# A two-layer encoder with a routed mixture of experts: two weight loads put into the buffers of w_o, and two groups of small TensorE products put elsewhere in the router stage

## The chip, the core and the metric

The kernel runs on one core of a Trainium2 chip. The metric is the device time of one execution in microseconds (us). TensorE (PE) does the matmuls and the transposes, VectorE (DVE) and ScalarE (ACT) the elementwise work, GpSimd (POOL) issues the gathers, the scatters and some stores, and SyncE (SP) issues the loads of all large weights.

## The reference

Two layers (DEPTH = 2) over 512 tokens of width 1024, float32. Each layer is an attention mixer followed by a mixture of experts; the part around the change is the passage from the one to the other:

```python
x = x + g1 * hybrid_mixer(h, ...)            # ends in: merged @ w_o
h = rms_norm(x, norm2[l]) * (1.0 + sc2) + sh2
x = x + g2 * grouped_moe(h.reshape(B * S, D), w_router, router_bias, w1[l], w3[l], w2[l])
```

`grouped_moe` scores 16 experts for each token, takes the best two inside the best group of four, and adds up `(silu(xb @ w1[e]) * (xb @ w3[e])) @ w2[e]` with the normed scores as weights. The six modulation vectors (sh1, sc1, g1, sh2, sc2, g2) of a layer are products of `silu(c)` with `w_ada[l]`.

## The kernel before, in words

**Stages of a layer.** Norm and transposes, input projection, two attentions, gates, the product with w_o (L2012, eight groups k = 0 to 7 of eight matmuls, two halves of the columns for each of four token tiles t), the router, and then the experts in 11 passes (PASSES) of 128 token rows. All is written out by hand, engine by engine; each engine runs its own list in order and waits on semaphores.

**Between w_o and the first pass.** DVE adds the mixer's output to x (L1405), PE transposes x and makes the router's logits, ACT writes the last tile of the scaled x (L1101) and POOL stores each tile of it to the DRAM tensor `xn_d` (L860), 512 KB each; the gathers read it. DVE turns the logits into one-hots (L1466), PE adds them up to ranks (L2048 to L2050, semaphore `ranks_ready`), DVE makes from the ranks the 128-wide indicator rows of the first pass (L1489, eight of them), PE multiplies them with token numbers (`slot_table(1, ...)`, L2059, 16 matmuls of 2 columns), and DVE writes the result as an index list (L1503, L1504, semaphore `ft_s`). With it POOL gathers the first pass's tokens from `xn_d` (L869). DVE then orders the experts by their counts (L1514, semaphore `ord_s`, which SP waits for before it loads any expert that depends on the order) and makes the indicator rows for all passes (L1541, semaphore `ds_s`); PE multiplies them (`slot_table(PASSES, ...)`, L2059, 16 matmuls of 22 columns) and DVE writes the full index table (L1545, L1548, semaphore `tb_s`), with which POOL gathers passes 1 and 2 and later ones. For a gathered pass PE transposes the tokens (`token_transposes`, L2073, two groups of four), ACT scales and shifts them into `xsT` (L1110), and the up products follow (L2107), then the down products (L2118).

**Modulation columns.** In layer 0 alone, PE also makes the next layer's first two modulation vectors by 16 one-column products (`next_mod`, L2037; each float32 product stands in the trace as two instructions). DVE reads them at L1572.

**POOL's list** at this place: wait for the four stores (`xn_st`), wait for `ft_s`, wait for x (`x1`), gather 0; wait for `tb_s`, gathers 1 and 2.

**Weight buffers.** The ring has six buffers of 2 MB (0 to 5); `hT` and `reg_a`, when they are free, serve as buffers 6 and 7. `MOE_LOADS` lists all 48 loads of a layer as (place, matrix, buffer), matrix 0, 1, 2 for w1, w3, w2. The places 0 and 1 are two fixed experts, whose loads wait for nothing but the buffer; the other places are filled in the order of the counts. The two halves of w_o lie in buffers 4 and 5: groups k = 0, 2, 4, 6 read buffer 4 and k = 1, 3, 5, 7 buffer 5. `hT` is read by the router's partial logits (L1991). `wo_r` counts the groups of w_o that are done, `lp4_r` the tiles with partial logits.

Of the kernel before, what the change touches and what calls it, by code (L numbers as in the profile page):

```python
# [16 lines left out]
NT = SEQ // P  # L17
NC = D // P
# [33 lines left out]
PASSES = 11  # L52
STATIC = (11, 12)
# [15 lines left out]
def rows_by_rank():  # L69

    first, rows = [None] * E, [0] * E
    for p, tiles in enumerate(TILES):
        for j, at, n in tiles:
# [4 lines left out]

MOE_LOADS = ((0, 2, 0), (1, 0, 1), (1, 2, 2), (0, 0, 3), (0, 1, 5), (1, 1, 6),
# [7 lines left out]
MOE_SLOT = {(j, m): s for j, m, s in MOE_LOADS}  # L89

TR_N1, TR_QK, TR_LAT, TR_KR, TR_N2, TR_X0 = 0, 8, 13, 18, 28, 36
# [21 lines left out]
def gathers(b):  # L113
    return (PASSES + 1 - b) // 2
# [65 lines left out]
def trunk(nc, x_in, c_in, w_ada, b_ada, norm1, w_in, q_norm_a, k_norm_a, q_a_norm, kv_norm, w_q_b,  # L180
# [27 lines left out]
    with ExitStack() as ctx:  # L208
# [253 lines left out]
        wo_r = sem("mixer_out_ready")  # L462
# [56 lines left out]
        def wait(eng, s, value):  # L519

            eng.wait_ge(s, value)
            eng.sem_inc(ticks, 1)
# [23 lines left out]
        def _(sp):  # L546
# [31 lines left out]
            for l in range(DEPTH):  # L578
# [58 lines left out]
                def load_w1(j, e):  # L637
                    s = MOE_SLOT[j, 0]
                    sp.dma_start(slot(s, NC, F), w1_v[l * E + e]).then_inc(w_rdy[s], 16)

                def load_w3(j, e):
                    s = MOE_SLOT[j, 1]
                    sp.dma_start(slot(s, NC, F), w3_v[l * E + e]).then_inc(w_rdy[s], 16)
# [8 lines left out]
                load_w2(1, STATIC[1])  # L652
                wait(sp, yb_r, l * 8 + 8)
                load_w1(0, STATIC[0])
                wait(sp, wo_r, l * 8 + 8)
                load_w3(0, STATIC[0])
                wait(sp, lp4_r, l * NT + NT)
                load_w3(1, STATIC[1])

                wait(sp, ord_s, l + 1)  # L660
# [7 lines left out]
                wait(sp, xn_st, l * 64 + 64)  # L668
                load_w1(2, rank[2])
                wait(sp, xg_s[0], l * (16 * gathers(0)) + 16)  # L670
                load_w3(2, rank[2])
                rank[3] = expert_at(3)
                wait(sp, h1_r, l * PASSES + 1)
# [1027 lines left out]
        def _(pe):  # L1701
# [46 lines left out]
            for l in range(DEPTH):  # L1748
# [280 lines left out]
                def next_mod(first, end):  # L2029

                    if l < DEPTH - 1:
                        if first == 0:
                            pe.wait_ge(nu_s, l * NX + NX)
                            pe.wait_ge(x1, l * 8 + 8)
                        for i in range(first, end):
                            m, c = i // NC, i % NC
                            ins = pe.matmul(bank[7][:, i:i + 1], nx_acc[:, m * D + c:(m + 1) * D:NC],  # L2037
                                            ones[:, 0:1], start=True, stop=True)
                        if end == 2 * NC:
                            ins.then_inc(nm_r, 1)  # L2040
# [7 lines left out]
                    pe.matmul(bank[3][:, (t + 1) * E:(NT + 1) * E], ones_b, before(t, NT - t), start=t == 0, stop=False)  # L2048
                pe.matmul(bank[3][:, E:NT * E], utri_b, ra_b[:, E:NT * E], start=False, stop=True)
                pe.matmul(bank[3][:, 0:E], utri_b, ra_b[:, 0:E], start=True, stop=True).then_inc(rk_r, 1)  # L2050
                next_mod(5, 2 * NC)

                def slot_table(n, slots, per_token, slots_done, done):

                    for q in range(2 * NT):
                        if slots_done is not None:
                            pe.wait_ge(slots_done, l * (2 * NT) + (q + 1))
                        for w in (0, 2):
                            ins = pe.matmul(bank[2][:, 0:2 * n], slots[:, q, :], per_token[:, q, w:w + 2, :].rearrange("p w n -> p (w n)"),  # L2059
                                            start=q == 0 and w == 0, stop=q == 2 * NT - 1 and w == 2)  # L2060
                    ins.then_inc(done, 1)
                slot_table(1, first_slot, places_b, fs_s, ft_r)
                slot_table(PASSES, slot_of, chosen, ds_s, tp_r)

                def token_transposes(g, p0, b, first=False):

                    xv = xg[:, b, :].rearrange("p (q c) -> p c q", c=NC)
                    for k in range(2):  # L2070
                        pe.wait_ge(tr_e, g + (k - 1))
                        for c in range(4):
                            ins = pe.transpose(bank[(p0 + k) % 2][:, c * P:(c + 1) * P], xv[:, 4 * k + c, :], ident)  # L2073
                        ins.then_inc(tr_r, 1)
# [46 lines left out]

                pe.wait_ge(xg_s[0], l * (16 * gathers(0)) + 16)
                token_transposes(l * TR + TR_X0, 0, 0)
                for p in range(PASSES):
                    g = l * TR + (TR_X0 + 2 + 3 * p)
                    if p == 4:
                        most = rows_beyond(pe, l)
                    pe.wait_ge(tr_e, g - 1)
                    for m, done in ((0, h1_r), (1, h3_r)):
                        if p == PASSES - 1 and m == 1:  # L2130
                            pe.wait_ge(tr_e, g)
                            pe.wait_ge(y_e, (l * PASSES + p - 1) * 2)
                            down_tiles(p - 1)
                        for j in places(p):
                            loaded(j, m)
                        for c in range(NC):
                            if p == 0 and c == 4:
                                pe.wait_ge(tr_e, g)
                            ins = up_tiles(p, m, 4 + m, c)
                        ins.then_inc(done, 1)  # L2140
                    if p + 1 < PASSES:
                        pe.wait_ge(xg_s[(p + 1) % 2], l * (16 * gathers((p + 1) % 2)) + 16 * ((p + 1) // 2 + 1))
                        token_transposes(g, p % 2, (p + 1) % 2)
                    if p == 1:
                        pe.wait_ge(wa_s, l + 1)
                        for t in range(NT):
                            ins = pe.transpose(bank[2][:, t * P:(t + 1) * P], last_a[:, t, :], ident)
                        ins.then_inc(wt_r, 1)
                    if 1 <= p < PASSES - 1:
                        pe.wait_ge(tr_e, g)  # L2150
                        if p >= 2:
                            pe.wait_ge(y_e, (l * PASSES + p - 1) * 2)
                        down_tiles(p - 1)
                    pe.wait_ge(u_s_s, l * PASSES + p + 1)
                    gu = g + 2 if p + 1 < PASSES else g
                    pe.wait_ge(tr_e, gu - 1)
                    hidden_transposes(p % 2).then_inc(tr_r, 1)
# [46 lines left out]
```

## Time and profile before

| what | value |
|---|---|
| median of 3 runs | 1566.89 us (1565.07 to 1570.05) |
| profiled execution | 1566.08 us |
| its span, first to last instruction | 1563.8 us |
| PE busy | 1476.5 us, 94% |
| DVE busy | 580.3 us, 37% |
| ACT busy | 428.0 us, 27% |
| moved by DMA | 346.80 MB, mean 222 GB/s |

A share of the span says which engine has most to do over all stages, and not what a stage waits for; that is read from the chain of work that ended last and from the engines' timelines. In a row of a timeline the first number is the start in us from the span's start, the second how long the row lasts; behind it the idle time of the engine before it and what ended it. Layer 0's router stage lies at about 507 to 532 us, layer 1's at about 1264 to 1288 us.

### The profile page before, as it was taken

The numbers are of one execution on the slowest core, as the hardware profiler recorded it, in microseconds if no ns is written. First come the engines' busy times: TensorE is split into PE (matmuls) and PEld (weight loads), VectorE is DVE, ScalarE is ACT, GpSimd is POOL, SyncE is SP. The second block draws the span as 40 slices with busy tenths as digits, with TensorE's granted clock in tenths as the row PEclk, the third lists the DMA queues.
The fourth block names the chain that finished last, engine by engine and source line by source line (L and its number), as shares of the span: only waits on it lengthen the run. The fifth ranks groups of instructions, "written<-read, shape, count | busy, mean of one in ns | idle before, by whom it ended". The sixth has DMA issues, their size and how long they took to land.

```text
span 1563.8 us, 20111 instructions
## 1 busy us (share of the span) xinstructions
PE 1476.5 (94%) x7800; PEld 800.5 (51%) x7801; DVE 580.3 (37%) x1379; ACT 428.0 (27%) x988; POOL 86.8 (6%) x96
## 2 busy tenths in 40 slices
PE   4998999999999799999899899999999959999997
PEld 1564565677754433343346555666776433334333
DVE  0056654575742511111154464463333251111115
ACT  1326564400011121211142565551000121121112
POOL 0000002000000001010000000020000010111000
PEclk8999999999999699999999999999999979999999
DMA  9625163225181889999972442601203458999994
GB/s 361 236 83 190 56 205 119 86 76 162 54 306 49 312 354 396 415 422 419 375 294 108 137 137 74 197 1 41 81 27 128 168 210 325 405 408 421 424 414 193
DMA packets 94874, 346.80 MB, mean 222 GB/s; under 512 B 13738, under 2 KB 37898, under 8 KB 80376
## 3 DMA queue, kind: packets, MB, share of 16 engines
q1 hardware_dynamic: 69152, 305.68, 50.5%
q0 software_dynamic: 8976, 31.40, 5.5%
q10 hardware_dynamic: 16648, 8.40, 1.9%
q8 instruction: 64, 1.05, 0.3%
q14 instruction: 34, 0.28, 0.0%
HBM read 331.55 MB, written 21.00 MB: 225 GB/s over the span
## 4 chain that ended last, share of the span: by engine, by line
PE 87%; DMA 6%; ACT 2%; DVE 2%; issue 1%; SPq 0%; DVEq 0%; POOLq 0%; ACTq 0%
PE bank L2107 18%; PE bank L1844 12%; PE bank L1794 10%; PE bank L2118 9%; PE bank L2012 7%; PE bank L1886 7%; PE bank L1901 5%; PE bank L1911 4%; PE bank L1921 4%; DMA hT<-in_w 3%; PE bank L1827 2%; PE bank L1723 2%; PE bank L1758 2%; DMA ring<-in_w_ada 1%; PE bank L2073 1%
## 5 line engine op out<-in xcount | busy, mean ns | idle before, releaser
L2107 PE MATMUL bank<-ring,reg_b 128*32 128x512 f32 (+2 forms) x1440 | 283.7, 606 | 2.9 <-ACT reg_b L1110 2.9
L2107 PEld LDWEIGHTS bank<-ring,reg_b 128*32 128x32 f32 (+2 forms) x1440 | 95.4, 127 | 158.3 <-issue 154.1
L1794 PE MATMUL bank<-ring,hT 128*128 128x512 f32 (+3 forms) x512 | 159.1, 472 | 2.4 <-ACT hT L943 2.4
L2118 PE MATMUL bank<-ring,reg_b 128*32 128x512 f32 (+2 forms) x640 | 141.3, 594 | 6.7 <-DMA hT<-in_w 3.7
L1794 PEld LDWEIGHTS bank<-ring,hT 128*128 128x128 f32 x512 | 97.8, 192 | 59.1 <-issue 32.2
L1886 PE MATMUL bank<-reg_a,ring 128*128 128x512 f32 x256 | 112.6, 593 | 0.9 <-issue 0.9
L2012 PE MATMUL bank<-ring,reg_b 128*128 128x512 f32 x256 | 113.0, 596 | 0.0
L1110 ACT ACTIVATE reg_b<-bank,cur 128x128 f32<-128x128 f32 x176 | 63.7, 467 | 170.5 <-PE bank L2073 170.5
L1022 ACT ACTIVATE reg_f<-bank,nmax 128x512 f32<-128x512 f32 x128 | 87.0, 684 | 61.5 <-DVE nmax L1320 60.5
L1320 DVE TENSOR_REDUCE nmax<-bank 128x1 f32<-128x512 f32 x128 | 83.8, 686 | 50.9 <-PE bank L1901 50.9
L1844 PE MATMUL bank<-hT,ring 128*128 128x256 f32 x384 | 88.1, 379 | 0.0
L2118 PEld LDWEIGHTS bank<-ring,reg_b 128*32 128x32 f32 (+2 forms) x640 | 48.3, 128 | 76.7 <-issue 72.9
L1620 DVE TENSOR_TENSOR reg_d<-bank,reg_c 128x512 f32<-128x512 f32 x44 | 30.4, 692 | 138.6 <-PE bank L2118 138.4
L1844 PEld LDWEIGHTS bank<-hT,ring 128*128 128x128 f32 x384 | 72.8, 190 | 15.8 <-issue 6.7
L1921 PE MATMUL bank<-cst,reg_f 128*128 128x128 f32 x512 | 71.2, 281 | 6.7 <-DVE reg_f L1314 4.1
L1886 PEld LDWEIGHTS bank<-reg_a,ring 128*128 128x128 f32 x256 | 48.5, 190 | 55.6 <-issue 54.9
L2012 PEld LDWEIGHTS bank<-ring,reg_b 128*128 128x128 f32 x256 | 47.7, 190 | 56.3 <-issue 56.3
L1608 DVE TENSOR_TENSOR reg_b<-bank,reg_b 128x512 f32<-128x512 f32 x22 | 15.2, 692 | 164.8 <-ACT reg_b L1117 164.8
L2107 PE MATMUL bank<-hT,reg_b 128*32 128x512 f32 (+1 forms) x160 | 70.5, 593 | 0.0
L1314 DVE TENSOR_SCALAR reg_f<-reg_f,linv 128x512 f32<-128x512 f32 x128 | 66.2, 517 | 10.3 <-issue 0.4
L1921 PEld LDWEIGHTS bank<-cst,reg_f 128*128 128x128 f32 x512 | 55.0, 141 | 25.9 <-DVE reg_f L1314 16.3
L1613 DVE TENSOR_TENSOR reg_b<-bank,reg_b 128x512 f32<-128x512 f32 x22 | 15.2, 692 | 123.6 <-PE bank L2107 123.6
(301 smaller groups left out, 1839.3 us busy)
## 6 DMA issues: line engine op xcount, KB each, us to landing
ring<-in_w SPq DMA_DIRECT2D x72, 2048.0 KB, 17.1
ring<-in_w_ada SPq DMA_DIRECT2D x19, 2048.0 KB, 7.8
hT<-in_w SPq DMA_DIRECT2D x12, 2048.0 KB, 14.5
reg_a<-in_w SPq DMA_DIRECT2D x12, 2048.0 KB, 13.5
ring<-in_w_in SPq DMA_DIRECT2D x10, 2048.0 KB, 15.7
vb<-in_w_ada ACTq DMA_DIRECT2D x16, 512.0 KB, 4.0
ring<-in_w_o SPq DMA_DIRECT2D x4, 2048.0 KB, 9.7
ring<-in_w_proj_a SPq DMA_DIRECT2D x8, 512.0 KB, 11.5
```

What stands on the lines that cost most here:

```text
L1022: A(prob[:, u % 2, h, :], bank[4 + at][:, :], ACT.Exp, bias=nmax[:, at:at + 1], accum_out=lsum[:, at:at + 1]).then_inc(ex_s, 1)
L1110: ins = A(xsT[:, b, cc, :], bank[(p0 + k) % 2][:, c * P:(c + 1) * P], ACT.Identity, scale=scale2(cc), bias=shift2(cc))
L1314: TS(prob[:, u % 2, h, :], prob[:, u % 2, h, :], linv[:, at:at + 1], None, ALU.mult).then_inc(pn_s, 1)
L1320: v.tensor_reduce(nmax[:, at:at + 1], bank[4 + at][:, :], X, ALU.max, negate=True).then_inc(mx_s, 1)
L1794: ins = pe.matmul(bank[z_bank(k)][:, 0:n], hT[:, c, t * P:(t + 1) * P], w[:, c, :], start=c == 0, stop=c == NC - 1)
L1844: ins = pe.matmul(bank[bk][:, half * 256:(half + 1) * 256], w[:, c, :], tokens[:, c, :], start=c == 0, stop=c == 3)
L1886: ins = pe.matmul(branch_bank(j, q)[:, :], w[:, c, (j % 4) * P:(j % 4 + 1) * P], oT[:, c + 4 * q, :], start=c == 0, stop=c == 3)
L1901: pe.matmul(bank[4 + 2 * (u % 2) + h][:, :], q_of(k, h), k_of(k, h), start=True, stop=True).then_inc(s_r, 1)
L1921: ins = pe.transpose(bank[2 + h][:, kc * P:(kc + 1) * P], prob[:, u % 2, h, kc * P:(kc + 1) * P], ident)
L2012: ins = pe.matmul(wo_bank(k)[:, :], mT[:, c, t * P:(t + 1) * P], w[:, c, :], start=c == 0, stop=c == NC - 1)
L2107: ins = pe.matmul(bank[bk][at:at + n, :], xsT[:, p % 2, c, at:at + n], slot(MOE_SLOT[j, m], NC, F)[:, c, :], start=c == 0, stop=c == NC - 1)
L2118: ins = pe.matmul(bank[6 + h][at:at + n, :], uT[:, c, at:at + n], slot(MOE_SLOT[j, 2], 4, D)[:, c, h * 512:(h + 1) * 512], start=c == 0, s ...
```

## The change

Three edits.

1. **Fixed matrices.** w3 of fixed place 0 goes to buffer 4 instead of 5, w3 of fixed place 1 to buffer 5 instead of 6 (`hT`), and w3 of place 2 to buffer 6 instead of 4. The other entries follow by the same exchange of names (5 becomes 4, 6 becomes 5, 4 becomes 6), so that each load still takes the place of the same matrix as before. SP's waits follow: w3 of place 0 waits for seven groups of w_o and not eight, w3 of place 1 for eight groups and not for the partial logits, and w3 of place 2 waits for the partial logits as well as for gather 0.
2. **Modulation columns.** `next_mod(5, 2 * NC)` stands behind the first pass's table and not ahead of it.
3. **Full table.** The products of the full table stand behind `token_transposes` of the first pass and not ahead of it.

```diff
-MOE_LOADS = ((0, 2, 0), (1, 0, 1), (1, 2, 2), (0, 0, 3), (0, 1, 5), (1, 1, 6),
-             (2, 0, 7), (2, 1, 4), (3, 0, 3), (3, 1, 5), (2, 2, 1), (4, 0, 7),
+MOE_LOADS = ((0, 2, 0), (1, 0, 1), (1, 2, 2), (0, 0, 3), (0, 1, 4), (1, 1, 5),
+             (2, 0, 7), (2, 1, 6), (3, 0, 3), (3, 1, 4), (2, 2, 1), (4, 0, 7),
...
                 load_w1(0, STATIC[0])
+                wait(sp, wo_r, l * 8 + 7)
+                load_w3(0, STATIC[0])
                 wait(sp, wo_r, l * 8 + 8)
-                load_w3(0, STATIC[0])
-                wait(sp, lp4_r, l * NT + NT)
                 load_w3(1, STATIC[1])
 
                 wait(sp, ord_s, l + 1)
...
                 wait(sp, xg_s[0], l * (16 * gathers(0)) + 16)
+                wait(sp, lp4_r, l * NT + NT)
                 load_w3(2, rank[2])
...
                 pe.matmul(bank[3][:, 0:E], utri_b, ra_b[:, 0:E], start=True, stop=True).then_inc(rk_r, 1)
-                next_mod(5, 2 * NC)
...
                 slot_table(1, first_slot, places_b, fs_s, ft_r)
-                slot_table(PASSES, slot_of, chosen, ds_s, tp_r)
+                next_mod(5, 2 * NC)
...
                 pe.wait_ge(xg_s[0], l * (16 * gathers(0)) + 16)
                 token_transposes(l * TR + TR_X0, 0, 0)
+                slot_table(PASSES, slot_of, chosen, ds_s, tp_r)
                 for p in range(PASSES):
```

PE in layer 0, from the ranks to the first up product, before. The rows of 128x1 are the modulation columns, 128x64 to 128x16 the ranks, 128x2 the first pass's table, 128x22 the full table, L2073 the transposes of the gathered tokens:

```order
L2037 MATMUL bank<-ones,reg_d 128x1 x5
L2048 MATMUL bank<-reg_f,cst 128x64
L2048 MATMUL bank<-reg_f,cst 128x48
L2048 MATMUL bank<-reg_f,cst 128x32
L2048 MATMUL bank<-reg_f,cst 128x16
L2049 MATMUL bank<-reg_f,cst 128x48
L2050 MATMUL bank<-reg_f,cst 128x16
L2037 MATMUL bank<-ones,reg_d 128x1 x11
L2059 MATMUL bank<-cst,reg_f 128x2 x16
L2059 MATMUL bank<-reg_f 128x22 x16
L2073 MATMUL bank<-cst,reg_b 128x128 x8
L2107 MATMUL bank<-ring,reg_b 32x512 x35
```

The same place of the changed kernel, whose lines stand one lower:

```order
L2038 MATMUL bank<-ones,reg_d 128x1 x5
L2049 MATMUL bank<-reg_f,cst 128x64
L2049 MATMUL bank<-reg_f,cst 128x48
L2049 MATMUL bank<-reg_f,cst 128x32
L2049 MATMUL bank<-reg_f,cst 128x16
L2050 MATMUL bank<-reg_f,cst 128x48
L2051 MATMUL bank<-reg_f,cst 128x16
L2059 MATMUL bank<-cst,reg_f 128x2 x16
L2038 MATMUL bank<-ones,reg_d 128x1 x11
L2073 MATMUL bank<-cst,reg_b 128x128 x8
L2059 MATMUL bank<-reg_f 128x22 x16
L2107 MATMUL bank<-ring,reg_b 32x512 x64
```

The eleven one-column products have moved behind the first table, and the full table's sixteen behind the transposes. In layer 1, which has no such columns, only the second of these holds.

SP's loads around the end of w_o, with their waits, before (`mixer_out_ready` is `wo_r`, `partial_logits_ready` is `lp4_r`, `expert_order_ready` is `ord_s`, `normed_stored` is `xn_st`, `tokens_gathered0` is gather 0):

```order
L639 DMA ring<-in_w1 128x4096 [waits proj_b_ready]
L643 DMA ring<-in_w3 128x4096 [waits mixer_out_ready]
L643 DMA hT<-in_w3 128x4096 [waits partial_logits_ready]
L665 TENSOR_LOAD order_i [waits expert_order_ready]
L665 ISA x2
L639 ISA [waits normed_stored]
L639 DMA reg_a<-in_w1 128x4096
L643 DMA ring<-in_w3 128x4096 [waits tokens_gathered0]
```

And of the changed kernel:

```order
L639 DMA ring<-in_w1 128x4096 [waits proj_b_ready]
L643 DMA ring<-in_w3 128x4096 [waits mixer_out_ready] x2
L665 TENSOR_LOAD order_i [waits expert_order_ready]
L665 ISA x2
L639 ISA [waits normed_stored]
L639 DMA reg_a<-in_w1 128x4096
L643 DMA hT<-in_w3 128x4096 [waits tokens_gathered0,partial_logits_ready]
```

Both fixed w3 now wait for groups of w_o alone, and the load that goes to `hT` is that of place 2.

## Rows read from the trace of the kernel before

**Rows 1.** The page, part 4: the chain that ended last, by engine.

```profile
PE 87%; DMA 6%; ACT 2%; DVE 2%; issue 1%; SPq 0%; DVEq 0%; POOLq 0%; ACTq 0%
```

**Rows 2.** The chain in layer 0's router stage: start us, us, what.

```profile
513.60 9.20 DMA xn_d<-reg_a
...
522.82 0.02 POOLq L522
...
522.92 0.02 POOLq L522
...
523.93 5.27 DMA reg_b<-xn_d,table
```

**Rows 3.** The chain in layer 1's router stage.

```profile
1271.06 8.19 DMA xn_d<-reg_a
...
1280.33 5.23 DMA reg_b<-xn_d,table
...
1288.38 2.77 PE bank L2107 x9
```

**Rows 4.** SP's timeline in layer 0 (issues of loads).

```profile
506.63 0.34 SPq L643 DMA_DIRECT2D ring<-in_w  x1
511.18 0.33 SPq L643 DMA_DIRECT2D hT<-in_w  x1
525.44 0.36 SPq L639 DMA_DIRECT2D reg_a<-in_w  x1
```

**Rows 5.** DMA issues of 495 to 496 us: KB each, us to landing.

```profile
xn_d<-reg_a POOLq DMA_DIRECT2D x1, 512.0 KB, 2.9
```

**Rows 6.** DVE's timeline in layer 0.

```profile
519.57 0.43 DVE L1499 TENSOR_TENSOR reg_f<-reg_f,cst 128x256 f32<-128x256 f32 x1
...
521.70 0.15 DVE L1504 TENSOR_SCALAR table<-bank 128x1 int32<-128x1 f32 x1
...
527.43 1.39 DVE L1541 TENSOR_SCALAR reg_f<-cst,reg_f 128x128 bf16<-128x128 bf16 x8
```

**Rows 7.** DVE's timeline in layer 1.

```profile
1277.36 0.42 DVE L1499 TENSOR_TENSOR reg_f<-reg_f,cst 128x256 f32<-128x256 f32 x1
...
1277.93 0.15 DVE L1504 TENSOR_SCALAR table<-bank 128x1 int32<-128x1 f32 x1
```

**Rows 8.** PE's timeline in layer 0.

```profile
499.41 7.11 PE L2012 MATMUL bank<-ring,reg_b 128*128 128x512 f32 x16
...
515.80 5.36 PE L2037 MATMUL bank<-ones,reg_d 128*128 128x1 f32 x22
521.01 0.57 PE L2059 MATMUL bank<-cst,reg_f 128*128 128x2 bf16 x16
527.74 1.37 PE L2059 MATMUL bank<-reg_f 128*128 128x22 bf16 x16 [6.16 <-DVE reg_f L1541]
529.25 1.97 PE L2073 MATMUL bank<-cst,reg_b 128*128 128x128 f32 x8
532.02 9.28 PE L2107 MATMUL bank<-ring,reg_b 128*32 128x512 f32 x67 [0.80 <-ACT reg_b L1110]
...
547.67 1.16 PE L2073 MATMUL bank<-cst,reg_b 128*128 128x128 f32 x8
```

**Rows 9.** Gather 1 of layer 0 in POOL's timeline.

```profile
530.57 1.03 POOL L869 DMA_INDIRECT reg_b<-xn_d,table  x1 [5.55 <-issue]
```

**Rows 10.** The same gather among the DMA issues of 530 to 531 us.

```profile
reg_b<-xn_d,table POOLq DMA_INDIRECT x1, 10.9
```

**Rows 11.** A load issued at 626.11 us, among DMA issues.

```profile
hT<-in_w SPq DMA_DIRECT2D x1, 2048.0 KB, 10.3
```

**Rows 12.** PE's timeline late in layer 0's experts.

```profile
763.03 0.62 PE L2118 MATMUL bank<-ring,reg_b 128*32 128x512 f32 x2 [1.83 <-DMA hT<-in_w]
```

**Rows 13.** Busy time by stretch: us; PE, PEld, DVE, ACT, POOL; clock; DMA share, GB/s.

```profile
511.80:535.60 23.80, 14.93 (x97) 11.41 (x101) 18.73 (x97) 4.13 (x10) 3.63 (x4) 0.50 0.77 292
1269.60:1293.30 23.70, 10.00 (x70) 5.12 (x74) 19.32 (x101) 3.78 (x9) 3.61 (x4) 0.50 0.83 314
```

12 rows, old and new, of the table MOE_LOADS are left out of this document.

## The prediction

> **What bounds the kernel now.** The chain of work that ended last lies on PE for 87% [rows 1], so a change counts only where PE stands still, or where its list gets shorter. This one removes no product. I therefore looked in the chain for the place that the edits touch. There it leaves PE for more than 15 us in each layer: ACT writes the last tile of the scaled x, POOL stores it, and the store takes 9.20 us in layer 0 and 8.19 us in layer 1 [rows 2, 3]; 1.1 us later POOL issues gather 0, which takes 5.27 and 5.23 us; then come PE's transposes (529.25) and, behind ACT's scaling, the up products (532.02) [rows 8]. So the gather waits for the store and not for its index list. The list is ready at 521.85 us in layer 0 (L1504, 521.70 and 0.15), the store at 522.80; in layer 1 it is 1278.08 against 1279.25 [rows 2, 3, 6, 7]. The list is the next thing to end that wait, 0.95 and 1.17 us earlier.
>
> **Why the store is slow.** SP issues a 2 MB load at 506.63 and another at 511.18 us [rows 4], and the store follows at 513.60. The store of the tile before it, with no load under way, took 2.9 us [rows 5].
>
> **The fixed matrices.** After the change the two loads wait for groups 7 and 8 of w_o. One group lasts 7.1 us and the seventh ended at about 499.5 [rows 8], so they go out at about 499.5 and 506.6 us. The load of 506.63 took the DMA engines from then to about 513: the next one was already behind it and no queue was free. With the second load where the first was, DMA is free at about 513 us and the store, issued at 513.60 as before, should land at 516.5; in layer 1, issued at 1271.06, at 1274.0. Were the load still under way for a microsecond, nothing would change, since the index list is the later one by 3.8 us. The matrices themselves are needed from 532 us on and gain nothing. What is late next is `ft_s`. The third moved load, w3 of place 2, keeps its wait for gather 0, and the partial logits are long done.
>
> **The modulation columns.** In layer 0 the eleven products (22 instructions) hold PE for 5.36 us, and the first table's products begin only at 521.01, 0.57 us long [rows 8]. DVE has its own work until 520.00 (L1499, 519.57 and 0.43) and then waits for them [rows 6]. With the columns behind the table, the products follow DVE's indicator rows directly, and DVE goes on 0.08 us after L1499, as it does in layer 1 (1277.78 to 1277.86) [rows 7]. The first list write moves from 521.62 to 520.08, and all that follows on DVE by 1.54 us: `ft_s` comes at 520.31 instead of 521.85. In layer 1 there are no columns and `ft_s` stays at 1278.08. The columns themselves now run from about 518.7 to 524.1; they are hidden as long as the gathered tokens come later, which they do by 2.5 us.
>
> **Gather 0.** POOL needed 1.13 us from the store's landing to the issue, with three waits in a row, one each 0.10 us [rows 2]. The index list stands second, so 1.03 us remain: gather 0 goes out at 521.34 in layer 0 and, by the same count with layer 1's 1.08 us, at 1279.06. It moves by 2.6 and 1.27 us. For its duration I keep 5.25 us, though the next load comes a little later behind it than before (w1 of place 2 was issued 1.5 us after the gather, 525.44 [rows 2, 4], and will be 2.4 us after it). The upper bound of what this is worth is 5.25 less 2.9, the same amount of data as a plain store alone, 2.3 us for each layer; a gather by single rows will not reach that, and before the change most of it ran ahead of the load anyway. I take 0.
>
> **The full table.** Before, PE stood ahead of this table for 6.16 us and paid 1.37 us for it, paced by DVE's eight indicator rows (L1541, 1.39 us) [rows 6, 8]. It ended at 529.11 and gather 0 landed at 529.20, so it would become the last wait as soon as the gather is earlier: unmoved, its DVE work would end at 527.3 and the gathered tokens lie there at 526.6, a loss of 0.8 us. Behind the transposes it needs no DVE any more. Its sixteen products then cost 0.6 us, like the sixteen of the first table at the same clock (0.57 us), at most the 1.37 us. They lie in the 0.80 us in which PE waits for ACT's first four tokens' parts [rows 8]. I take 0 for the cost; the bound is 0.6 us for each layer. What gets later is the table itself and gathers 1 and 2. In layer 0 it is ready some 2.8 us after the transposes begin, at 529.4, as before. Gather 1 went out at 530.57 and took 10.9 us [rows 9, 10], and the transposes that need it began at 547.67 [rows 8]; they will begin at 545.1, 3.5 us after it lands. In layer 1 gather 1 goes out some 2 us later than now and has about 4 us left.
>
> **The sum.** Gain 2.6 us in layer 0 and 1.3 us in layer 1, 3.9 us. Against the profiled execution's own 1566.08 us that gives 1562.2 us. The median of the runs shown is 0.8 us above that execution, so against the median the change would look like 4.7 us, just at 0.3%, which is about what a measurement of this kernel can tell from no change.
>
> **Does the gain last?** The experts' passes are full of loads, and late in them PE waits for loads (1.83 us for one) [rows 12]. If the queue of loads ran at its own pace from the start, an earlier PE would only wait longer there. But in pass 4 a load still lands 10.3 us after its issue [rows 11], about as one at the start of the experts, and its issue waits for PE. The queue is not yet behind there, and it moves with PE. I take the late waits as unchanged, give or take 1 us.
>
> **The clock.** PE has 0.50 of its clock (1.2 GHz) up to 535.6 us in layer 0 and 1293.3 us in layer 1 [rows 13], that is 3.6 us after the first up product in layer 0 (532.02) and 4.9 us in layer 1 (1288.38) [rows 3, 8]. The columns' 5.36 us at that level did not bring the clock back. Half the difference, 0.7 us for each layer, is what comes and goes without any edit. The Trainium skill, in TensorE: Matmul & The Clock Gate, Part 1, says that how much work passes before the clock returns varies from run to run of one kernel; the two layers here agree.
>
> **Rivals.**
> - *More than the sum: the gather gets faster*, because it has the DMA engines for itself. For it: its 5.25 us are 2.3 us more than the plain store. Against it: the load behind it was issued 1.5 us later. At half of the bound it is 1.2 us for each layer, 1559.8 us. Chance 0.12. The Trainium skill, in DMA: Bandwidth & Descriptors, Anatomy of one DMA, gives about 2.0 us and bytes over 436 GB/s for a transfer issued by GpSimd; that makes 3.2 us for 512 KB as an estimate, near the 2.9 us of the store, and with it the gain would be 8 us and not 3.9.
> - *Part of the gain is given back*, because the loads keep their own pace: in layer 1 the first load in expert order waits for `ord_s`, which doesn't move there, and in layer 0 that moves 1.54 us. Then 1.5 us remain, 1564.5 us. Chance 0.20.
> - *The change doesn't do what it says:* the last tile's store is slow for another reason than the loads, and still lands at 522.8 and 1279.2. Then nothing is gained: 1566.1 us. Against it is the store that took 2.9 us. Chance 0.05. A rule of the Trainium skill speaks for it: in DMA: Bandwidth & Descriptors, Queues, rings and completion order, each DMA engine takes turns between the queues that have work, packet by packet. By that rule the store would have needed no more than about twice its 2.9 us beside a load, as an estimate, and the trace with 9.20 us does not agree.
> - *Slower:* gathers 1 and 2, now behind the transposes, come too late for pass 1. They have 3.5 and 4 us. To end 0.3% above the median, both gathers 1 would have to land some 8 us later than I reckon, 19 us after their issue instead of 10.9. Chance 0.03; it would give 1571 us or more.
>
> **How the numbers follow.** The forecast holds 0.60, with 1562.2 us. Its own range is 1560.5 (0.3 us quicker gathers and 0.7 us of clock) to 1564. About four tenths of it lie below 0.3%, which with the faster gather makes 0.36 for faster; slower has 0.04 with what I have not thought of, the rest, 0.60, is no measurable change. The range for 8 in 10 takes in the faster gather and the rival that gives part back, and the scatter of the runs of about 1 us: 1559.3 to 1566.2 us.
>
> **What would show it.** Right: the last tile's store lands in about 3 us; gather 0 is issued 1.0 us behind L1504 in both layers; no idle time on DVE ahead of L1503; the full table's products within the gap before the first up product; that product about 2.6 us earlier in layer 0 and 3.9 us in layer 1, from the span's start. Wrong: a store above 6 us, a wait of PE for gather 1, an up product that waits for the table, or late waits for loads that have grown by what was gained.

## The result, and the profile after

| | before | changed |
|---|---|---|
| median | 1568.74 us (7 runs, 1563.92 to 1571.72) | 1558.95 us (7 runs, 1557.89 to 1561.6) |
| profiled execution | 1566.08 us | 1557.89 us |
| ratio to the kernel before, on record | | 0.9941, 95% interval 0.9919 to 0.9962 |

The change makes the kernel some 9 us faster where 3.9 us were forecast (9.3 us by the ratio; it is an estimate of its own and not the quotient of the two medians, which is 0.9938 and gives 9.8 us). The median lies 0.35 us below the low end of the range.

The changed kernel's page, part 4, the chain by engine:

```profile
PE 89%; DMA 3%; DVE 3%; ACT 3%; issue 1%; DVEq 0%; SPq 0%; ACTq 0%; POOLq 0%
```

DMA has lost half of its share. Its chain in layer 0's router stage (start us, us, what) answers to [rows 2]:

```profile
517.45 0.08 DVE table L1505
...
518.57 4.17 DMA reg_b<-xn_d,table
522.78 1.13 PE bank L2073 x4
...
525.55 6.83 PE bank L2107 x53
```

And in layer 1, to [rows 3]:

```profile
1274.16 4.46 DMA reg_b<-xn_d,table
1278.67 1.13 PE bank L2073 x4
...
1281.44 4.75 PE bank L2107 x25
```

The store is gone from both chains; DVE's index list (L1505) stands in its place, and the gather follows it by 1.04 us in layer 0 and 0.98 us in layer 1. The gather itself takes 4.17 and 4.46 us and not 5.27 and 5.23. SP's and POOL's timelines in layer 0, for [rows 4, 9]:

```profile
495.89 8.72 SPq L643 DMA_DIRECT2D ring<-in_w  x2
521.12 0.36 SPq L639 DMA_DIRECT2D reg_a<-in_w  x1
```

```profile
510.85 0.53 POOL L861 DMA_DIRECT2D xn_d<-reg_a  x1 [17.47 <-ACT reg_a L1102]
518.57 1.09 POOL L870 DMA_INDIRECT reg_b<-xn_d,table  x1 [7.19 <-issue]
526.62 1.03 POOL L870 DMA_INDIRECT reg_b<-xn_d,table  x1 [6.96 <-issue]
```

Both w3 loads are out by 504.6 us. The DMA issues of 510.5 to 511 us (KB, us to landing) give the last tile's store, for [rows 5]:

```profile
xn_d<-reg_a POOLq DMA_DIRECT2D x1, 512.0 KB, 2.9
```

PE's timeline in layer 0, for [rows 8]:

```profile
514.57 1.35 PE L2059 MATMUL bank<-cst,reg_f 128*128 128x2 bf16 x16 [1.39 <-DVE reg_f L1490]
515.78 5.37 PE L2038 MATMUL bank<-ones,reg_d 128*128 128x1 f32 x22
522.78 1.97 PE L2073 MATMUL bank<-cst,reg_b 128*128 128x128 f32 x8 [1.63 <-DMA reg_b<-xn_d,table]
524.54 0.62 PE L2059 MATMUL bank<-reg_f 128*128 128x22 bf16 x16
525.55 1.08 PE L2107 MATMUL bank<-ring,reg_b 128*32 128x512 f32 x4 [0.39 <-ACT reg_b L1111]
```

The columns end 1.6 us before the gathered tokens are there, and the full table takes 0.62 us inside PE's wait for ACT: the first up product comes 2.77 us behind the first transpose, before and after. Stretches of the changed kernel, for [rows 13] (us; PE, PEld, DVE, ACT, POOL; clock; DMA share, GB/s):

```profile
509.90:526.80 16.90, 11.73 (x81) 10.22 (x85) 13.83 (x74) 3.19 (x9) 1.80 (x3) 0.50 0.48 180
1267.60:1284.50 16.90, 7.18 (x62) 4.35 (x66) 13.08 (x64) 2.91 (x8) 3.11 (x3) 0.50 0.54 195
526.90:543.90 17.00, 15.07 (x138) 5.01 (x132) 6.40 (x28) 3.70 (x10) 2.72 (x3) 1.00 0.97 385
543.95:547.30 3.35, 3.35 (x10) 0.92 (x9) 0.00 (x0) 0.24 (x1) 0.00 (x0) 0.50 0.96 410
```

PE is at half clock for 17 us and no longer 24 in each layer. In layer 0 the clock falls once more, at the start of pass 1, where it did not before, and again at 741.9 us, each time for 3.4 us.

**Where the 8.2 us between the two profiles lie.** I measure the *stage* from DVE's first instruction on the last group of w_o to the first up product, and the *first pass* from there to the first product of L2093 (transposes ahead of the down products).

| piece | before | changed | difference |
|---|---|---|---|
| up to the stage, layer 0 | 506.56 | 503.80 | -2.8, nothing was edited there |
| stage, layer 0 | 25.46 | 21.75 | -3.7 |
| first pass, layer 0 | 18.05 | 16.90 | -1.2 |
| from there to the stage of layer 1 | 713.94 | 716.66 | +2.7; the two stretches at half clock, at 544 and 742 us, would be some 3.3 by themselves |
| stage, layer 1 | 24.37 | 22.34 | -2.0 |
| first pass, layer 1 | 18.74 | 17.82 | -0.9 |
| the rest | 256.7 | 256.3 | -0.3 |

So the stages give 5.7 us and the first passes 2.1 us. That leaves two questions: why the gathers got shorter, and why the median of before lies so far above the execution profiled first.

### The profile page after: what moved, and what is told of

The parts are those of the page before. It is cut to its first block, busy times and chain, and to the rows that moved or that the text cites. A ratio compares the mean times of both kernels' runs of the same rounds, so it can differ in the third digit from the quotient of the medians.

```text
span 1555.6 us, 20113 instructions
## 1 busy us (share of the span) xinstructions
PE 1474.0 (95%) x7800; PEld 798.0 (51%) x7801; DVE 579.8 (37%) x1379; ACT 428.2 (28%) x988; POOL 86.8 (6%) x96
## 4 chain that ended last, share of the span: by engine, by line
PE 89%; DMA 3%; DVE 3%; ACT 3%; issue 1%; DVEq 0%; SPq 0%; ACTq 0%; POOLq 0%
PE bank L2107 19%; PE bank L1845 12%; PE bank L1795 10%; PE bank L2118 10%; PE bank L2013 7%; PE bank L1887 7%; PE bank L1902 5%; PE bank L1912 4%; PE bank L1922 4%; PE bank L1828 2%; PE bank L1724 2%; PE bank L1759 2%; DMA ring<-in_w 1%; PE bank L2073 1%; DMA ring<-in_w_ada 1%
## 5 line engine op out<-in xcount | busy, mean ns | idle before, releaser
L2107 PE MATMUL bank<-ring,reg_b 128*32 128x512 f32 (+2 forms) x1312 | 269.0, 602 | 2.1 <-ACT reg_b L1111 2.1
L2107 PEld LDWEIGHTS bank<-ring,reg_b 128*32 128x32 f32 (+2 forms) x1312 | 86.4, 125 | 139.7 <-issue 136.9
L2118 PE MATMUL bank<-ring,reg_b 128*32 128x512 f32 (+2 forms) x768 | 143.0, 603 | 6.1 <-ACT reg_b L1111 2.6
L2118 PEld LDWEIGHTS bank<-ring,reg_b 128*32 128x32 f32 (+2 forms) x768 | 47.2, 124 | 79.9 <-issue 74.5
L2107 PE MATMUL bank<-hT,reg_b 128*32 128x512 f32 (+2 forms) x288 | 84.6, 593 | 0.0
L1922 PEld LDWEIGHTS bank<-cst,reg_f 128*128 128x128 f32 x512 | 54.6, 140 | 26.3 <-DVE reg_f L1315 16.9
```

Source lines behind the costliest of these rows:

```text
L1922: ins = pe.transpose(bank[2 + h][:, kc * P:(kc + 1) * P], prob[:, u % 2, h, kc * P:(kc + 1) * P], ident)
L2107: ins = pe.matmul(bank[bk][at:at + n, :], xsT[:, p % 2, c, at:at + n], slot(MOE_SLOT[j, m], NC, F)[:, c, :], start=c == 0, stop=c == NC - 1)
L2118: ins = pe.matmul(bank[6 + h][at:at + n, :], uT[:, c, at:at + n], slot(MOE_SLOT[j, 2], 4, D)[:, c, h * 512:(h + 1) * 512], start=c == 0, s ...
```

## The experiments

The theory for e1 to e4: the three edits are links of one chain. Its rival: each brings a share of its own. The table has the stage and gather 0 in each profile (layer 0 / layer 1, us) and the ratio to the kernel before of the same comparison, as it is on record, with its interval.

| kernel | stage | gather 0 | w1 load issued behind gather 0 | first pass | ratio |
|---|---|---|---|---|---|
| before, first profile | 25.5 / 24.4 | 5.27 / 5.23 | 1.51 / 1.11 | 18.1 / 18.7 | |
| changed, first profile | 21.8 / 22.3 | 4.17 / 4.46 | 2.55 / 2.35 | 16.9 / 17.8 | 0.9941 (0.9919 to 0.9962) |
| e1 loads only | 25.2 / 23.7 | 4.31 / 4.52 | 2.55 / 2.35 | 18.7 / 19.0 | 0.9970 (0.9958 to 0.9982) |
| e2 no loads | 29.1 / 28.9 | 9.57 / 9.35 | 0.59 / 0.69 | 17.9 / 18.0 | 1.0012 (0.9997 to 1.0026) |
| e3 no columns | 23.4 / 22.2 | 4.23 / 4.31 | 2.55 / 2.36 | 17.9 / 18.0 | 0.9939 (0.9915 to 0.9963) |
| e4 no table | 23.6 / 23.7 | 4.14 / 4.39 | 2.55 / 2.36 | 19.0 / 17.6 | 0.9954 (0.9939 to 0.9969) |
| e5 before, second | 31.3 / 29.1 | 10.42 / 9.49 | 0.80 / 0.67 | 19.0 / 18.1 | one run |
| e6 before, w1 held | 25.2 / 23.8 | 4.51 / 4.38 | behind its landing | 18.5 / 19.2 | 0.9982 (0.9970 to 0.9994) |
| e7 load on gather | 29.6 / 29.5 | 11.98 / 11.61 | another 0.5 / 0.9 ahead | 18.2 / 18.0 | 1.0037 (1.0017 to 1.0058) |
| e8 warm, 2 and 8 | 23.5 / 23.3 | 4.29 / 4.41 | 2.54 / 2.35 | 16.3 / 16.3 | 0.9939 (0.9923 to 0.9955) |
| e9 changed, second | 21.8 / 22.1 | 4.26 / 4.25 | 2.56 / 2.36 | 16.8 / 16.8 | 0.9938 (0.9923 to 0.9952) |
| e10 warm, 0 and 4 | 21.9 / 22.0 | 4.31 / 4.50 | 2.54 / 2.36 | 16.9 / 16.3 | 0.9950 (0.9932 to 0.9967) |
| e11 one load | 22.7 / 22.6 | 4.54 / 4.34 | 2.20 / 1.95 | 17.8 / 17.6 | one run |
| e12 before, third | 25.2 / 29.5 | 4.48 / 10.01 | 2.27 / 0.81 | 18.8 / 18.3 | one run |

**e1, the moved loads alone.** The changed kernel with edits 2 and 3 undone:

```diff
+                next_mod(5, 2 * NC)
...
                 slot_table(1, first_slot, places_b, fs_s, ft_r)
-                next_mod(5, 2 * NC)
+                slot_table(PASSES, slot_of, chosen, ds_s, tp_r)
...
                 token_transposes(l * TR + TR_X0, 0, 0)
-                slot_table(PASSES, slot_of, chosen, ds_s, tp_r)
```

> The moved loads alone (edit 1); columns and full table stand as before. My theory: the edits are links of one chain, so this one alone brings almost nothing though its store is quick. The last tile's store lands in about 3 us in both layers and gather 0 goes out 1.0 us behind L1504; but PE cannot transpose before the full table's products, which end with DVE's indicator rows at the old place. From the last group of w_o (DVE's L1402 of k = 7) to the first up product: 25.4 us in layer 0 (before 25.5, after the change 21.8) and 23.9 us in layer 1 (before 24.4, after 22.3). Whole kernel 0.5 us faster than before. The rival, that each edit brings a share of its own, expects about 23 us in both layers and 3 us off the kernel.

The stages came out as the theory has them. PE's timeline in layer 0:

```profile
526.11 1.36 PE L2060 MATMUL bank<-reg_f 128*128 128x22 bf16 x16 [6.16 <-DVE reg_f L1542]
527.35 1.94 PE L2074 MATMUL bank<-cst,reg_b 128*128 128x128 f32 x8
```

The gathered tokens had landed at 525.57, and PE still stood before the table. But the whole kernel gained 4.7 us by the ratio, not 0.5 us. Two numbers of the same run that don't fit: 1564.9 us is 1.2 us below the 1566.08 us of the first profile of before, and 4.8 us below the median of before, 1569.75 us. The missing part had to be in the kernel before.

**e2, edits 2 and 3 without the loads.** The change's first edit undone, as in the diff of the change read backwards.

> Edits 2 and 3 without the moved loads. Theory: the store again takes 8 to 9 us beside the two loads, gather 0 goes out 1.1 us behind its landing, and the stage from w_o to the first up product is 25.5 and 24.4 us as before, give or take 0.2; the kernel takes the time of before. Rival, that the last tile's store is slow for another reason that the loads don't set: the store is quick in some runs whatever the loads do, or the stage gets shorter by 1.5 us in layer 0 through the index list. On the clock: if it came back sooner because transposes and table stand together, the half-clock stretch is 17 us here too instead of 24.

The store was slow again (8.56 and 8.60 us), and the whole kernel took the time of before within its interval, both as expected, but the stages grew to 29 us. Half clock lasted 24 us in both layers, so edits 2 and 3 do not bring it to 17 beside the late gather. The chain and SP's timeline in layer 1:

```profile
1284.00 9.35 DMA reg_b<-xn_d,table
```

```profile
1284.69 0.35 SPq L639 DMA_DIRECT2D reg_a<-in_w  x1
```

The gather took 9.35 us with the load of w1 of place 2 issued 0.69 us behind it. In the first profile of before the same load came 1.11 us behind, and the gather took 5.23 us. SP's timeline of before in layer 1:

```profile
1281.44 0.35 SPq L639 DMA_DIRECT2D reg_a<-in_w  x1
```

That made a new theory, the race: gather 0 and the first load in expert order are issued within a microsecond, by two engines, off two signals (the store's landing and `ord_s`), and a 2 MB load that comes soon enough holds the gather up.

**e3, no columns; e4, no table.** The changed kernel with edit 2 undone, and with edit 3 undone:

```diff
+                next_mod(5, 2 * NC)
...
-                next_mod(5, 2 * NC)
```

```diff
+                slot_table(PASSES, slot_of, chosen, ds_s, tp_r)
...
-                slot_table(PASSES, slot_of, chosen, ds_s, tp_r)
```

> Edits 1 and 3, the modulation columns again ahead of the first table. Theory: only layer 0 differs from the changed kernel. Its index list is late by 1.5 us, since DVE waits for PE at L1503, and all behind it: stage 23.3 us in layer 0, 22.3 in layer 1. 1.5 us slower than the changed kernel. Rival, that the columns were hidden: 21.8 us in layer 0.

> Edits 1 and 2, the full table's products again ahead of the transposes. Theory: gather 0 lands as in the changed kernel, 4.2 to 4.5 us after its issue, but PE waits for DVE's last indicator row; transposes start at once behind the table. Stage 23.9 us in layer 0 and 24.0 in layer 1 (changed kernel 21.8 and 22.3), so 3.8 us slower than the changed kernel. On the clock: if PE's work close together brought it back sooner, the half-clock stretch is again 24 us and another 1 us is lost in each first pass; if it was chance, it is 17 or 20 us as often as not.

Stages as expected to 0.3 us in both. For e3 the whole kernel shows nothing of the 1.5 us that were expected (its median is 0.3 us above the changed kernel's, its ratio 0.0002 below), and its six runs, 1558.2 to 1564.1 us, could not tell it; in the profile the 1.6 us are in layer 0's stage alone. e4 is slower than the changed kernel by 4.0 us by the medians and 2.0 us by the ratios, whose intervals overlap; its two stages are 3.3 us longer. Half clock lasted 24 us in its layer 0 and 20 in layer 1, which decides for neither of the two outcomes that the expectation names. For the stages the theory holds: edit 1 alone takes 0.3 and 0.6 us off them (e1), edits 2 and 3 alone take nothing off (e2), and all three take 3.7 and 2.0 us. PE's timeline of e4, layer 0:

```profile
523.29 1.37 PE L2059 MATMUL bank<-reg_f 128*128 128x22 bf16 x16 [2.28 <-DVE reg_f L1542]
```

**e5 and e12, the kernel before profiled again.**

> The kernel before, unchanged, profiled once more. Theory of the race: gather 0 takes 4.2 to 5.3 us when it is issued 1.1 us or more ahead of the 2 MB load of w1 of place 2, and 9 to 10 us when that load is issued 0.7 us or less behind it; the kernel before stands at 1.1 to 1.5 us by the first profile and crosses to the slow side when the store lands 0.4 us later. So in this profile at least one layer may show a gather of 9 us, with the kernel some 4 us slower than the 1566.1 us of the first profile. Rival, that the gather's length is fixed by the edits and not by the race: 5.2 us in both layers again.

> The kernel before, profiled a third time. The two profiles so far have no lost race (1566.1 us) and two lost races (1576.8 us). The median of its runs, 1568.5 to 1569.8 us, would be one lost race or less: I expect a gather of 9 to 10 us in one layer and 5 us in the other, or none. In each layer the gather is long exactly if the load is issued less than about 1 us behind it.

Both layers lost the race in e5 (1576.77 us), one in e12 (1569.63 us), none in the first profile (1566.08 us). The chain of e5 in layer 1, with SP's load:

```profile
1277.11 8.62 DMA xn_d<-reg_a
...
1286.81 9.49 DMA reg_b<-xn_d,table
...
1299.12 1.06 PE bank L2107
```

```profile
1287.48 0.35 SPq L639 DMA_DIRECT2D reg_a<-in_w  x1
```

e12 has both outcomes in one execution; POOL's and SP's timelines of layer 0, and of layer 1:

```profile
522.03 1.09 POOL L869 DMA_INDIRECT reg_b<-xn_d,table  x1 [9.02 <-issue]
524.30 0.36 SPq L639 DMA_DIRECT2D reg_a<-in_w  x1
```

```profile
1280.02 1.06 POOL L869 DMA_INDIRECT reg_b<-xn_d,table  x1 [9.04 <-issue]
1280.83 0.35 SPq L639 DMA_DIRECT2D reg_a<-in_w  x1
```

The first gather took 4.48 us, the second 10.01. A lost race costs its stage 4.7 to 5.8 us, set against the first profile. The median of before, 1568.5 to 1569.8 us over the comparisons, is near the time of e12, with one lost race. The executions without a profile can't be sorted this way, so how often each outcome comes is not shown.

The packets show how the gather is held up. In e12's layer 1, from 1283 to 1288 us (queue: packets, MB, share of the 16 DMA engines; q1 has SP's loads, q0 POOL's transfers):

```profile
q1 hardware_dynamic: 99, 1.62, 75.8%
q0 software_dynamic: 101, 0.41, 20.7%
```

The two queues take turns packet by packet, 101 against 99, but a packet of the gather has 4 KB and one of the load 16 KB. The gather so gets a fifth of the bytes and lands with the load, 1290.04 against 1290.21 us. In the first profile of before, layer 0, this is from 523.9 to 527.5 us:

```profile
q0 software_dynamic: 100, 0.41, 43.8%
```

Of the gather's 128 packets 100 had gone before the load, issued at 525.44, had one. In e12's layer 1 it was 10, and in both layers of e2 none.

**e6, the kernel before with the load held.** One edit:

```diff
                 wait(sp, xn_st, l * 64 + 64)
-                load_w1(2, rank[2])
                 wait(sp, xg_s[0], l * (16 * gathers(0)) + 16)
+                load_w1(2, rank[2])
```

> The kernel before with one edit: SP issues the load of w1 of place 2 only when gather 0 has landed. Race theory: the gather is alone on the DMA engines in both layers and takes 4.1 to 4.6 us instead of 5.2 or 9; the stage from w_o to the first up product is then bound by the full table in layer 0 (25.3 us) and 23.8 us in layer 1, and the kernel is 3 to 4 us faster than the median of before, like the moved loads alone (ratio 0.997). Pass 1 needs that load 20 us later and does not wait. Rival, that the load's place does not matter: no change, ratio 1.000.

Gathers of 4.51 and 4.38 us with the store as slow as before. The kernel gained 2.8 us by the ratio (0.9982 of 1568.45; 3.8 by the medians) where 3 to 4 us were expected, and its slowest run was 1568.2 us where the kernel before reached 1575.7. That is what the load's place is worth without any edit of the change: the race, and the small part by which the gathers of the first profile (5.27 and 5.23 us) are longer than these.

**e7, a load put on the gather.** The changed kernel with w3 of fixed place 1 loaded at the index list:

```diff
-                wait(sp, wo_r, l * 8 + 8)
+                wait(sp, ft_s, l + 1)
                 load_w3(1, STATIC[1])
```

> The changed kernel, but w3 of fixed place 1 is loaded when the first index list is ready, some 1 us ahead of gather 0. Race theory: the gather stands behind a 2 MB load and takes 9 to 10 us instead of 4.2 to 4.5; the first up product comes 5 us later in both layers, 10 us in all, and the kernel is as slow as before or slower. Rival, that the DMA engines take turns between queues packet by packet: the gather takes at most twice its 4.2 us less the start, some 6 us, and the kernel loses 3 us.

Chain and SP's timeline in layer 1:

```profile
1281.41 11.61 DMA reg_b<-xn_d,table
1293.07 1.13 PE bank L2073 x4
```

```profile
1280.51 0.33 SPq L643 DMA_DIRECT2D ring<-in_w  x1
1283.76 0.35 SPq L639 DMA_DIRECT2D reg_a<-in_w  x1
```

The load in front landed 8.0 us after its issue, at 1288.5, and the gather 4.5 us behind that. That 4.5 us is what a gather takes alone is chance, as the packets show, first from 1281.5 to 1285.9 us, then from 1286 to 1291.5:

```profile
q1 hardware_dynamic: 96, 1.57, 101.6%
```

```profile
q1 hardware_dynamic: 127, 1.82, 77.9%
q0 software_dynamic: 121, 0.50, 21.9%
```

The gather had no packet up to 4.7 us behind its issue, where alone it takes 1.8 us. Then its packets and those of the two loads went turn by turn, 121 against 127. The rival of the expectation, turns packet by packet, is therefore how these queues work here, and only its price of 6 us fails, since it takes the packets as equally large and the gather's start as undisturbed. The stages grew by 7.8 and 7.2 us, and the kernel by some 15 us where 10 were expected.

**e11, one load beside the store.** The changed kernel with the wait that w3 of place 1 had before:

```diff
-                wait(sp, wo_r, l * 8 + 8)
+                wait(sp, lp4_r, l * NT + NT)
                 load_w3(1, STATIC[1])
```

> The changed kernel, but w3 of fixed place 1 waits for the partial logits, as its buffer did before: one 2 MB load is under way when the last tile's store is issued, and not two. If the store stands behind what the loads' queue holds, it lands when that one load does, 6 to 7 us after its issue, still ahead of the index list (13.7 us behind w_o), and the stage stays at 21.8 and 22.3 us. Rival, turns between queues packet by packet: 4 to 5 us.

Chain and SP's timeline in layer 0:

```profile
510.94 7.13 DMA xn_d<-reg_a
```

```profile
508.51 0.33 SPq L643 DMA_DIRECT2D ring<-in_w  x1
```

The load landed at 517.16 and the store at 518.07. I had the store ahead of the index list, but it landed 0.46 us behind it, so the stage grew by 0.9 us, and in layer 1, where it landed 0.33 us behind the list, by 0.3 us. The store's first packet came 4.0 and 4.3 us behind its issue, against 1.1 us in the changed kernel. One load is enough to take the list's place.

**e8 and e10, unused products while PE waits for the gather.** The changed kernel with (numbers of e10; e8 had 2 and 8):

```diff
+                for i in range(0 if l < DEPTH - 1 else 4):
+                    pe.matmul(bank[5][:, :], ident, cst[:, 0:512], start=True, stop=True)
                 pe.wait_ge(xg_s[0], l * (16 * gathers(0)) + 16)
```

> The changed kernel with products that are not used, 128 x 512 into a bank that is free, while PE waits for gather 0: 2 in layer 0, 8 in layer 1. If the clock's return is set by how much PE does ahead of the first pass, it is back before the first up product in layer 1 (half-clock stretch 13 us or less instead of 17), the transposes take 1.2 us instead of 2.0, the first pass takes 16.6 us instead of 17.8, and 1 to 2 us come off the kernel against the changed one. Layer 0 has room for 1.6 us only and may gain 0 to 0.5 us. If the return is chance, the first pass stays at 17 to 18 us and the kernel takes the time of the changed one.

> The changed kernel with four unused products of 128 x 512, in layer 1 alone, while PE waits for gather 0. e8 showed that a product lasts 1.8 us at half clock and that its eight delayed the transposes by 1.6 us though the clock came back. Four last 5 to 7 us and the gather lands 7.5 us after PE is free: the transposes start on time (19.5 us behind the last group of w_o), take 1.2 us, the first up product comes at 22.0 us, and the first pass takes 16.3 us instead of 17.8. 1.5 to 2 us faster than the changed kernel. Rival, that the clock falls again while PE waits for the rest of the gather: no gain.

The clock does follow PE's work. In e8's layer 1 half clock lasted 10 us and the first pass took 16.3 us, but its products also held the transposes for 1.5 to 1.6 us in both layers. e10 avoided that; PE's timeline in layer 1:

```profile
1270.69 5.70 PE L2123 MATMUL bank<-cst 128*128 128x512 f32 x8
1278.32 1.16 PE L2073 MATMUL bank<-cst,reg_b 128*128 128x128 f32 x8 [1.93 <-DMA reg_b<-xn_d,table]
...
1280.69 2.78 PE L2107 MATMUL bank<-ring,reg_b 128*32 128x512 f32 x24 [0.82 <-ACT reg_b L1111]
```

The transposes started on time and took 1.16 us, and stage and first pass together took 38.3 us against 38.9 in e9. Yet the kernel was not faster: 1560.19 us against the 1558.77 us of e9 on the same chip. The expected gain of 1.5 to 2 us was reckoned from the changed kernel's first profile, where the clock came back 3.2 us behind layer 1's first up product. In e9 it came back 1.1 us behind it without any unused product, so only 0.6 us were left. In both profiles the clock then fell at the start of pass 1, at 1298.7 and 1298.2 us, for 3.4 us, which costs 1.7 us. No version here beats the changed kernel clearly.

**e9, the changed kernel again.**

> The changed kernel, unchanged, timed again beside the runs of e10 and profiled a second time. Race theory: the store lands 3 to 4 us ahead of the index list and the load of w1 of place 2 is issued 2.3 us or more behind gather 0, so the gather takes 4.2 to 4.5 us again in both layers and the runs scatter over 4 us at most. Stage 21.8 and 22.3 us as in its first profile, ratio 0.994. On the clock: the return behind the first up product may differ by 2 us from the first profile. Rival, that the changed kernel also loses the race at times: a gather of 9 us in a layer.

As expected: gathers of 4.26 and 4.25 us, six runs within 3.1 us. No gather with the next load 1.95 us or more behind it and none just ahead of it is long (changed, e1, e3, e4, e6, e8 to e11, and layer 0 of e12).

## Why the prediction was right in kind and too small

- **What bounds the stage: right.** The last tile's store ended the wait for gather 0, and the two loads made it slow: 2.9 to 3.8 us without them, 8.6 us with them (e2), 7.1 us with one (e11). One reading of the rows was off: 499.41 is where the eighth group of w_o begins, and the seventh ended 1 us earlier, so the first load went out 8.0 us ahead of the eighth group's end. That changed nothing.
- **How the loads slow it: in part wrong.** The prediction says that "no queue was free", and takes the 9.20 us as speaking against turns packet by packet. But of that store the first packet came 4.4 us behind the issue, against 1.1 us alone, and from 518 to 520 us 59 of its packets went beside 36 of the load. So there are two parts, a late start and turns of unequal size.
- **What is late next: right.** `ft_s`, with the gather 1.04 us behind L1505 where 1.03 was reckoned (layer 1: 0.98 and 0.98), and the columns' 1.54 us came as 1.6 us (the list is written 15.3 us behind w_o's last group before and in e3, and 13.7 us after).
- **The full table: right.** 0.62 us inside PE's wait for ACT, and 1.4 to 1.9 us lost in a stage when it is put back (e4). In layer 0 gather 1 landed 3.6 us before it was needed, where 3.5 were forecast. The late waits for loads did not grow: PE's waits for experts' weights are 5.4 us in the first profile of before, 2.1 us in the changed kernel and 4.7 us in e9.
- **The size of the stages: the term that was mis-sized is the gather's duration.** The prediction said "I keep 5.25 us", "before the change most of it ran ahead of the load anyway", and took 0 for what the next load's distance is worth. It is worth 1.10 us in layer 0 and 0.77 us in layer 1. With them the sum's 2.6 and 1.27 us become the 3.7 and 2.0 us of the profile. That most of it ran ahead of the load was true, 102 and 81 of its 128 packets; the rest went beside 23 and 16 packets of the load, and the last came 4.8 and 4.7 us behind the issue instead of 3.7 and 4.0. The rival *the gather gets faster* had the right sign, place and reason, with 1.2 us for each layer. Its 8 us for the whole gain lie near the measured 9 by luck, since they ask for a gather of 3.2 us, and none was shorter than 4.1 us.
- **The step that failed: the state of the kernel before.** The sum was made against one execution, and the 1.1 us between gather and load in layer 1 stood in the rows without my asking what a store 0.3 us slower would do. With 0.8 us or less the gather takes 9.4 to 10.4 us (e2, e5, e12: five of five stages, at 0.59 to 0.81 us), with 1.1 us or more, and no load in front, 4.1 to 5.3 us. The moved loads pull the store off that edge. Of the 9 us, the race's part is some 3 us as an estimate (e6: 2.8, which holds a little of the shorter gathers too; the median of before less its first profile: 2.7).
- **The clock: taken as chance, in part an effect.** With the table behind the transposes the clock came back 1.1 to 3.9 us behind the first up product, 2.7 in the mean of 13 stages (without those with unused products); with the table ahead of them 2.7 to 6.0 us, 4.7 in the mean of 12. The first pass took 17.6 us in the mean against 18.6. The pair that differs by edit 3 alone agrees (e1 18.7 and 19.0 us, e3 17.9 and 18.0); against e4 the changed kernel is 2.1 us shorter in layer 0 and 0.2 us longer in layer 1. So edit 3 gives about 1 us for each layer there in the mean, not in every stage. About half of it is given back: of those 13 stages five had a fall of the clock at the start of pass 1 (1.7 us each, 0.65 us in the mean), of the other 12 one. In these 25 the fall came exactly where the clock was back within 2.9 us of the first up product (six of six) and never where it took 3.1 us or more (none of nineteen). Why was not tried.

## What to carry to other kernels

When the chain runs through a small transfer that one engine issues while another issues a large load off its own signal, look at the distance between the two issues, in every profile to be had: within a microsecond the outcome changes from run to run, and a single execution shows one side of it. Count the packets of both queues too: turns are by packet, so the transfer with the smaller packets loses. Put large loads where no small transfer on the chain is waiting, even if nobody needs them early. And make such edits together: here moving the columns without moving the loads brought layer 0's next load from 1.51 to 0.59 us behind the gather (e2) and gained nothing, while all three gave 9 us.

## What the runs showed of the hardware

- A 2 MB load of SP's queue and a 512 KB transfer of POOL's take turns packet by packet, and the turns are unequal in bytes: 99 packets with 1.62 MB against 101 with 0.41 MB in 5 us (e12, layer 1). The Trainium skill, in DMA: Bandwidth & Descriptors, Queues, rings and completion order, has each DMA engine take turns between queues packet by packet; the trace agrees, and adds that here one queue's packet has 16 KB and the other's 4 KB.
- Issue and first packet lie apart, and by different times. A gather with no load in its way has its first packet 1.8 us behind its issue, a store of 512 KB 1.1 us, and a 2 MB load 1.0 to 1.4 us (2.1 and 2.5 us in the first profile of before, which is open). So a load issued 0.6 to 0.8 us *later* has its first packet 1.6 to 2.1 us behind the gather's issue, when 0 to 10 of the gather's 128 packets have gone; issued 1.1 us later or more, its first came at 3.4 us or more, when 81 to 128 had gone.
- A POOL transfer issued while loads are under way starts late as well: the store 3.9 to 4.6 us behind its issue (before, e2, e5, e6, e11, e12), the gather 4.5 and 4.7 us in e7 and 3.4 to 4.1 us in e2 and e5's layer 1. What it waits for is open.
- PE's busy time alone does not tell when its clock comes back. In the changed kernel's layer 0 the eleven one-column products kept PE busy for 5.37 us without a gap, and it stayed at half clock (1.2 GHz) for another 5.7 us. In e10's layer 1 four float32 products of 128 x 512, 5.70 us, stood at the same place, and half clock lasted 10 us instead of 17.
